# Turning the residual stream into rows on VectorE, in 32x32 blocks, instead of on TensorE

## The reference, cut to what matters

```python
def conv_ffn(x, prev, up, cw, cb, down):
    a = x @ up
    gate, val = jnp.split(a, 2, axis=-1)
    gc, new = causal_conv(gate, prev, cw)
    h = jax.nn.gelu(gc + cb, approximate=True) * val
    return h @ down, new
# in block():
    x = x + rmsnorm(mix, g_mix_post)                      # this is x1
    f, new_ffn = conv_ffn(rmsnorm(x, g_ffn_pre), ffn_prev, ffn_up, ffn_conv_w, ffn_conv_b, ffn_down)
    x = x + rmsnorm(f, g_ffn_post)                        # the output y
```

## Time and profile before

| what | us |
|---|---|
| median of 3 runs (lowest, highest) | 1357.12 (1356.16, 1357.23) |
| the profiled execution, its own time | 1358.99 |
| its span | 1357.3 |
| TensorE busy in the span | 1332.5 (98%) |
| VectorE busy | 758.4 (56%) |
| ScalarE busy | 502.1 (37%) |
| GpSimd busy | 104.6 (8%) |

### The profile page before, as it was taken

The page is one execution under the profiler, slowest core; times in us unless marked ns, Lnnn a source line. Parts: engine busy times, 40 slices in busy tenths (PEclk is TensorE's granted clock), DMA queues, the critical chain, the costliest instruction groups (busy, mean ns, idle before and its releaser), DMA issues.

```text
span 1357.3 us, 24741 instructions
## 1 busy us (share of the span) xinstructions
PE 1332.5 (98%) x9026; PEld 1320.5 (97%) x9026; DVE 758.4 (56%) x1175; ACT 502.1 (37%) x727; POOL 104.6 (8%) x215
## 2 busy tenths in 40 slices
PE   5999999999999999999999999999999999999997
PEld 4999999999999999999999999999999999999996
DVE  6446855544458755544655554555555445656445
ACT  4323333333455433332333333333333333333652
POOL 4542000000014000000000000000000000000000
PEclk9999999999999999999999999999999999999999
DMA  8654455555563545456545545645544565554453
GB/s 222 162 155 137 118 149 142 145 153 152 140 179 94 155 131 152 124 149 188 149 130 155 143 128 149 186 135 155 155 135 129 149 174 155 155 145 135 112 150 114
DMA packets 379010, 199.59 MB, mean 147 GB/s; under 512 B 3924, under 2 KB 374592, under 8 KB 378968
## 3 DMA queue, kind: packets, MB, share of 16 engines
q1 hardware_dynamic: 378896, 198.83, 53.1%
q0 software_dynamic: 80, 0.31, 0.1%
HBM read 195.68 MB, written 3.56 MB: 147 GB/s over the span
## 4 chain that ended last, share of the span: by engine, by line
PE 95%; SPq 2%; DVE 2%; DMA 0%; issue 0%; ACT 0%; DVEq 0%; ACTq 0%
PE mm L491 30%; PE mm L492 30%; PE mm L495 30%; SPq L341 1%; PE tb L495 1%; PE tb L491 1%; PE tb L492 1%; PE tb L767 1%; DVE y_tok L1617 1%; DMA sgu_bias<-in_sgu_b_dram 0%; DVE a_lo L1431 0%; DVE f L1421 0%; SPq L355 0%; DVE up_lo L1148 0%; SPq L393 0%
## 5 line engine op out<-in xcount | busy, mean ns | idle before, releaser
L491 PE MATMUL mm<-a_hi,w_hi 128*128 128x320 f32 x1872 | 581.7, 311 | 0.0
L495 PE MATMUL mm<-a_lo,w_hi 128*128 128x320 f32 x1872 | 579.1, 309 | 1.8 <-DVE a_lo L1209 1.8
L492 PE MATMUL mm<-a_hi,w_lo 128*128 128x320 f32 x1872 | 578.6, 309 | 0.0
L867 ACT ACTIVATE w_hi<-raw 128x1024 fp32r (+3 forms) x384 | 352.8, 967 | 451.3 <-PE mm L495 431.0
L1160 DVE TENSOR_TENSOR w_lo<-raw,w_hi 128x1024 fp32r<-128x1024 f32 (+1 forms) x380 | 414.9, 1133 | 127.0 <-ACT w_hi L867 126.8
L495 PEld LDWEIGHTS mm<-a_lo,w_hi 128*128 128x128 f32 x1872 | 351.5, 188 | 2.8 <-DVE a_lo L1209 2.7
L491 PEld LDWEIGHTS mm<-a_hi,w_hi 128*128 128x128 f32 x1872 | 351.6, 188 | 1.2
L492 PEld LDWEIGHTS mm<-a_hi,w_lo 128*128 128x128 f32 x1872 | 351.6, 188 | 0.3
L495 PE MATMUL mm<-m_lo,w_hi 128*128 128x320 f32 x884 | 273.2, 309 | 0.0
L491 PE MATMUL mm<-h_hi,w_hi 128*128 128x320 f32 x660 | 205.7, 312 | 0.0
L492 PE MATMUL mm<-h_hi,w_lo 128*128 128x320 f32 x660 | 203.9, 309 | 0.0
(11 more groups left out here) (262 smaller groups left out, 914.5 us busy)
## 6 DMA issues: line engine op xcount, KB each, us to landing
raw<-in_ffn_up_dram SPq DMA_DIRECT2D x88, 1024.0 KB, 5.7
raw<-in_ffn_down_dram SPq DMA_DIRECT2D x60, 704.0 KB, 4.8
raw<-in_w_in_dram SPq DMA_DIRECT2D x34, 1024.0 KB, 5.6
raw<-in_w_out_dram SPq DMA_DIRECT2D x16, 1024.0 KB, 5.9
x_tok<-in_x_prompt_dram SPq DMA_DIRECT2D x4, 512.0 KB, 7.6
raw<-in_ffn_down_dram SPq DMA_DIRECT2D x2, 1024.0 KB, 6.2
out_dram<-y_tok SPq DMA_DIRECT2D x8, 256.0 KB
raw<-in_ffn_down_dram SPq DMA_DIRECT2D x1, 768.0 KB, 4.5
```

What stands on the lines that cost most here:

```text
L491: pe.matmul(out, whi[:, s], hi, start=start, stop=False)
L492: pe.matmul(out, wlo[:, s], hi, start=False, stop=False)
L495: return pe.matmul(out, whi[:, s], tile(lo, k), start=False, stop=stop)
L867: act.activation(w_hi[:, d:d + half], src, ACT.Copy).then_inc(w_hi_done, 1)
```

## The change

The x units leave TensorE and ScalarE. VectorE turns `xT` into `y_tok` itself with `dve.transpose`, from SBUF to SBUF, in 32 x 32 squares: one operation reads 32 partitions (32 channels of each of the 16 tiles, 32 tokens of each: 512 elements a partition) and writes 32 partitions (32 tokens) of `y_tok`, 16 pieces of 32 elements each. Ten groups of 32 tokens times four groups of 32 channels are 40 operations; four stand behind each of the chunks m = 0 to 9 on VectorE. ScalarE's piece 1 waits for all 40 (`x_blocks`) in place of `X_TURNED`.

```diff
-        UNITS = sorted([(m // 2, "x", m // 3, m % 3) for m in range(3 * QD)] +
-                       [((6, 6, 7, 9, 10, 11)[3 * k4 + i], "f", k4, i) for k4 in range(QD - 2)
+        UNITS = sorted([((6, 6, 7, 9, 10, 11)[3 * k4 + i], "f", k4, i) for k4 in range(QD - 2)
                         for i in range(3)] +
                        [(8, "state", n, 0) for n in range(2)])
         UNITS += [(WIDE, "f", QD - 2, i) for i in range(3)]
-        X_TURNED = 1 + max(n for n, u in enumerate(UNITS) if u[1] == "x")
+        BLOCKS = [(i, b, a) for i, (t0, nt) in enumerate(TT) for b in range(nt // 32) for a in range(P // 32)]
+        PER_CHUNK = 4
+        assert len(BLOCKS) <= PER_CHUNK * (WIDE - 2)
...
-                    src = xT if what == "x" else f
-                    if what == "f":
-                        pe.wait_ge(f_gained, 4 * k4 + 4)
+                    pe.wait_ge(f_gained, 4 * k4 + 4)
...
-                    if what == "x":
-                        act.activation(y_tok[0:nt, i, k4 * 512:(k4 + 1) * 512], bank[0:nt, :],
-                                       ACT.Copy).then_inc(taken, 1)
-                    elif what == "f":
+                    if what == "f":
...
                     if j == 1:
-                        act.wait_ge(turned, X_TURNED)
+                        act.wait_ge(x_blocks, len(BLOCKS))
...
+                def turn_block(i, b, a):
+
+                    t0 = TT[i][0] + 32 * b
+                    dve.transpose(
+                        y_tok[32 * b:32 * b + 32, i, :].rearrange("p (k c) -> p k c", c=P)[:, :, 32 * a:32 * a + 32],
+                        xT[32 * a:32 * a + 32, :].rearrange("p (k t) -> p k t", t=T)[:, :, t0:t0 + 32]
+                        ).then_inc(x_blocks, 1)
+
                 for m in range(WIDE):
                     add_down(qd + m // 2, m % 2, m)
...
                     else:
                         split_wide(m - WIDE + 2)
+                    for block in BLOCKS[PER_CHUNK * m:PER_CHUNK * m + PER_CHUNK]:
+                        turn_block(*block)
                 split_wide(2)
```

More of the change, by code:

```diff
@@ L261, in hybrid_layer @@
         turned = sem("turned")
+        x_blocks = sem("x_blocks")
         taken = sem("taken")
@@ L766, in turn_unit @@
                         o = (4 * k4 + k) * T + t0
-                        last = pe.transpose(bank[0:nt, k * P:(k + 1) * P], src[:, o:o + nt], ident[:, :])
+                        last = pe.transpose(bank[0:nt, k * P:(k + 1) * P], f[:, o:o + nt], ident[:, :])
                 last.then_inc(turned, 1)
```

## The result

The changed kernel takes 1350.15 us (median of 5 runs, 1349.61 to 1350.31) against 1357.12 (5 runs, 1356.16 to 1359.61): the ratio is 0.9947, 95% interval 0.9934 to 0.996, so 7.0 us faster. The forecast was 1352.8, and 7.0 is more than the 5.28 us that it called the ceiling. So the direction was right, and something outside the argument gave time as well. The profiled execution took 1349.61, its span is 1347.9.

What follows compares the result with a forecast made beforehand. TensorE, busy 98% of the span, was taken as the bound. Removing 5.28 us of transposes, less 1.0 us of new waiting for VectorE, gives 4.3 us: 1357.12 becomes 1352.8, range 1351.3 to 1362.

Steps and rivals of the forecast that it cites:

- the ceiling: Most the edit could gain: 5.28 us, all of the x units' time on TensorE's chain.
- What leaves TensorE: 48 transposes of `xT` in twelve units of 0.44 us leave TensorE's chain: 5.28 us.
- The price of a block: VectorE's step b from one 32 x 512 transpose to the next: 0.685 + 0.04 = 0.72 us, without overlap.
- rival C: VectorE becomes the bound: four-byte elements transpose at half rate, b = 1.22, 15.7 us slower; chance 0.20 including 0.90 to 1.22.
- The wait that takes its place: TensorE waits for low weights that VectorE makes behind the blocks: 1.0 us, leaving a net gain of 4.3.
- 40b - 27.8: TensorE's added wait in us, from VectorE's work 29.24 + 40b against 57.0 available; b is the step per block.
- the last deadline: Wide piece 0, needed behind chunk 11 and made behind all 40 blocks; called the tightest, 1.0 us of wait.
- the deadline that the forecast named as the lesser: Chunk 6, with 16 blocks ahead of it: some 0.5 of the 1.0 us wait comes earlier there, not added.
- The pace in the new profile: VectorE's `add_down` was to start every 4.84 us in chunks 1 to 3, without idle time before it from chunk 1.
- The other signs: Blocks' mean and step near 0.69 and 0.72 us; TensorE's `w_lo` waits under 1 us together, none for ScalarE or DMA.
- The knee: VectorE's room for blocks: no wait below b = 0.695, 1.0 us at 0.72, each 0.1 us in b is 4 us.
- The sum: Whole span 1357.3 - 4.3 = 1353.0; median 1357.12 becomes 1352.8.

Runs made afterwards that it cites:

- the kernel without blocks: Changed kernel with the 40 VectorE turns replaced by eight memsets of the same rows, x1 left out of the output; 1349.40 us, ratio 0.9942.
- the uneven deal: Changed kernel with the 40 turns dealt 3, 4, 4, 3, 3, 4, 4, 4, 4, 4, 3, 0 over the chunks; 1349.72 us, ratio 0.9944.
- padding on ScalarE or GpSimd: Changed kernel with twelve one-column copies at ScalarE's end, 1350.20 us; or with 96 more fulfilled waits at GpSimd's end, 1350.10 us.

## Why the prediction was right, and why it was wrong

**What leaves TensorE: right.** 5.28 us were forecast from the chain; the kernel without blocks gained 5.27 in the last quarter and the uneven deal 5.28.

**The price of a block: right.** Forecast 0.685 and a step of 0.72; measured 0.702 and (2.90 - 0.70) / 3 = 0.733. The blocks follow each other without overlap, where the tail's operations overlap by 0.07. That this hangs on where they start is in the rows above: in chunk 0 the first block reads and writes from partition 0 on, as `split_lo` does, and starts at 1260.08, 0.08 us before the low parts end (1258.47 + 1.69); in chunk 1 it writes another group of 32 partitions and starts at 1265.52, 0.02 after they end (1263.81 + 1.69). Chunks 4 (1281.80 against 1280.19 + 1.68) and 8 are as chunk 0, the others as chunk 1. The Trainium skill ("VectorE: DVE Perf Modes", "Two Vector instructions with no wait between them") says that an instruction whose input or output starts in another quadrant is held until all earlier ones have finished; the trace agrees. A block takes (702 - 160) / 512 = 1.06 ns an element beyond the 160 ns of a one-element operation, about the 1.04 by which the wide rows differ, so rival C is out. The Trainium skill ("Vector Engine (DVE) Microarchitecture Reference", "3.8 The reshape front-end and per-opcode configuration") has one element per cycle per lane for this transpose; the trace agrees, for four-byte elements too. By the estimate from the Trainium skill's table ("VectorE: DVE Perf Modes", "The three transpose paths") the step was 0.75, which is 0.02 high.

**The wait that takes its place: right in kind, twice too large, and at another deadline.** Forecast 1.0 us by 40b - 27.8, which with the measured 0.733 would be 1.5; measured 0.45. The step at fault is VectorE's own work per chunk, taken as 2.58 and 3.51 us from the earlier trace rows. These rows are of an engine that came early. There the low parts start 0.48 us after `add_square` (1269.15 to 1269.63), about when ScalarE's first half, begun at 1268.80, is ready, and the wide ones wait 0.26 us for ScalarE by their own row; once VectorE is behind, ScalarE is done, and the 0.48 is 0.40: 1263.41 to 1263.81. The chunk is 2.50 us and the wide one 3.15 (1311.90 to 1315.05). With these the same sum is 2.51 + 9 x 2.50 + 3.15 + 40 x 0.733 - 57.0 = 0.5 us. That it meets the 0.45 is in part luck, for this sum is of the last deadline, piece 0, and TensorE doesn't wait there: its one wait stands before chunk 6, the deadline that the forecast named as the lesser. (It gave "some 0.5" for it; by its own rows it is 2.51 + 4 x 2.58 + 16 x 0.72 - 23.67 = 0.7, where TensorE's 23.67 is 1291.42 - 1263.10, chunk 6's first matmul before, less 4.40 and 0.25.) Once chunk 6 has waited 0.46 us, piece 0 finds its low parts ready in time.

**The pace in the new profile: wrong in one sign.** `add_down` was to come every 4.84 us in chunks 1 to 3. It comes every 5.4, which is what the forecast's own 5.46 us of work in a chunk with no idle time says; TensorE's pace had been written for VectorE's. The other signs came: 0.702 and 0.733 for a block, TensorE's waits for `w_lo` under 1 us, none for ScalarE or DMA.

**The knee: right.** The forecast said that each 0.1 us in b is 4 us, with no wait below 0.695 and 1.0 us at 0.72, so that VectorE stands at the edge. Eight more blocks cost 5.70 of the 5.86 us that they last (8 x 0.733).

**What the sum left out: the start.** The step that failed is "The sum", which took the rest of the span for fixed and carried 4.3 us over to the median, and with it "nothing more than 5.28 us can be gained". It holds for the work that the edit touches. The other 2.2 us of the medians lie in the first 40 us, and they aren't an effect of turning blocks on VectorE or of freeing TensorE: sixteen idle waits give the kernel before 1.7 us of it (1356.46 beside it, 1354.80 with them), 108 take 1.9 from the changed one (1352.22 against 1350.33 with one wait, on the same chip), and padding on ScalarE or GpSimd does nothing. The edit changed TensorE's instruction list and happened upon one with an early start: 4.8 of the 7.0 us are earned and 2.2 are luck. The range from 1351.3 left out that the same work can start 2 us sooner or later in another build.

What is shown is this dependence, in ten TensorE lists with the start between 32.3 and about 36 us in the median, and that neither length nor executed work orders it. It is there by the first product, when TensorE has done no more than transpose `vec_raw` and `x_tok`. How the list gets to the landing of the first inputs isn't shown, and stays open. Where the instructions and the inputs lie in memory is a guess that no run here tests. The clock adds to the effect in some executions: a stretch at 1.2 GHz behind TensorE's idle time falls on the small transposes in one profile (1.49 us for six) and not in another (0.82), which was 1.6 of the 4.57 us. It isn't the cause alone, since the input's landing moved by 3.0 us.

## What to carry to other kernels

A ceiling for an edit holds for the stage it touches. Here 2 to 3 us at the start of the span came and went with changes of TensorE's instruction list that added no work, so compare kernels by a stretch between two instructions that both have, and test a surplus with idle instructions before explaining it. Idle time of a helper engine is a budget with a knee: 40 operations filled it here, and the next ones cost nearly their full length; dealing them unevenly, three in place of four in some early chunks and the last three behind piece 0, bought back the rest. Sum the work up to every deadline and not only to the last. A stretch of work read while the engine waits for others has those waits in it and shrinks once the engine is late.

## What the runs showed that was not expected

- Waits that are long fulfilled aren't free in number: with 313 of them at the end of TensorE's list there are 25.5 us from `rest` to the end in place of 20.7, so they held the span open for some 5 us.
- A float32 32 x 512 transpose on VectorE from SBUF to SBUF, strided at both ends and crossing from one group of 32 partitions to another, takes 0.702 us, hardly more than a plain copy of 512 out of PSUM (0.685).
- The start of the same program differs by up to 5 us between executions (33.0 to 38.1 for the kernel before, over four chips; 33.1 to 38.0 on one), while the 1220.8 us behind it agree to 0.1 in the two profiles.
